# Gate stage, out projection and pooling layer rewritten with features on the partitions; group mix multiplied into the value weights on chip

## The reference

```python
def adaln_params(c, w, b):
    shift, scale, gate = split(silu(c) @ w + b, 3)
# layer 0: sliding-window attention (window 128, 16 heads of 64, 4 kv heads), gate width 1024
    q, k, v, g = split(h @ w_in);  o = banded_sink_attention(rope(rms(q)), rope(rms(k)), v, sinks)
    branch = (o * silu(g)) @ w_out
# layer 1: causal pooling over trailing windows 2/4/8/16, one per group of 256 channels
    v, g = split(h @ w_in)                                   # 1024 + 1024
    pooled = window_sum(v) / count - v                       # per group
    mixed = einsum('bsgc,gcd->bsgd', pooled, w_group) * scale   # 256x256 per group
    branch = (mixed * silu(g)) @ w_out
x = x + gate * branch        # h = rms_norm(x, norm_g) * (1 + scale) + shift
```

## Time and profile before

| | |
|---|---|
| three timed runs | 1764.85, 1769.49, 1775.3 us; median 1769.49 |
| span of the profiled execution | 1762.8 us |
| its own time | not listed apart; the lowest of the timed runs is 2.1 us above the span, the median 6.7 |
| mean granted clock of PE | 0.961 |
| gate and out projection, pooling, last projection | 399.9, 469.0, 198.0 us |

### The profile page before, as it was taken

How to read it: one execution, slowest core, us unless ns; L and a number is a source line. 1 busy time by engine, 2 the same in 40 slices (tenths; PEclk the granted TensorE clock), 3 DMA queues, 4 the chain that set the end, 5 groups by cost and what they waited for, 6 DMA issues and landing times. The chain is left out here.

```text
span 1762.8 us, 27247 instructions
## 1 busy us (share of the span) xinstructions
PE 1581.6 (90%) x9964; PEld 1392.5 (79%) x9964; DVE 920.7 (52%) x1686; ACT 532.0 (30%) x1286; POOL 403.9 (23%) x472
## 2 busy tenths in 40 slices
PE   7579989999898984799999996699999999969998
PEld 3367777777777774699999994689999999957887
DVE  1467766777667763543333333664544545434333
ACT  0255555555555543411100011431221221121000
POOL 0225555555545552010000001111101111000000
PEclk9799999999999986899999998799999999989999
DMA  8331111111111102844333442530111101044332
GB/s 333 113 128 49 73 48 71 48 48 71 48 71 48 59 14 90 283 147 147 143 148 152 155 156 89 173 99 29 42 42 42 48 18 42 19 137 160 148 145 107
DMA packets 75507, 175.36 MB, mean 99 GB/s; under 512 B 11330, under 2 KB 41026, under 8 KB 70212
## 3 DMA queue, kind: packets, MB, share of 16 engines
q1 hardware_dynamic: 71268, 161.60, 25.3%
q0 software_dynamic: 4192, 13.12, 2.2%
HBM read 124.36 MB, written 50.34 MB: 99 GB/s over the span
## 5 line engine op out<-in xcount | busy, mean ns | idle before, releaser
L828 PE MATMUL at_proj<-w_qkv,at_ht 128*128 128x512 f32 x1152 | 286.7, 398 | 11.8 <-DVE at_ht L629 7.2
L828 PEld LDWEIGHTS at_proj<-w_qkv,at_ht 128*128 128x128 f32 x1152 | 211.4, 190 | 60.0 <-DVE at_ht L629 8.2
L1237 PE MATMUL gp_g_ps<-gp_ht,gp_w_g 128*128 128x256 f32 x1536 | 187.4, 285 | 15.7 <-DMA gp_ht<-ht_split 15.7
L1237 PEld LDWEIGHTS gp_g_ps<-gp_ht,gp_w_g 128*128 128x128 f32 x1536 | 187.0, 194 | 16.6 <-DMA gp_ht<-ht_split 16.0
L1630 PE MATMUL po_v_ps<-po_ht,po_w_vg 128*128 128x256 f32 x1536 | 191.3, 286 | 9.4 <-DVE po_ht L1506 9.4
L1630 PEld LDWEIGHTS po_v_ps<-po_ht,po_w_vg 128*128 128x128 f32 x1536 | 188.2, 194 | 11.2 <-DVE po_ht L1506 5.9
L1808 PE MATMUL pj_y_ps<-pj_w_o,pj_zs 128*128 128x512 f32 x768 | 180.6, 397 | 16.8 <-DVE pj_w_o L70 15.2
L1630 PE MATMUL po_g_ps<-po_ht,po_w_vg 128*128 128x256 f32 x1536 | 190.0, 283 | 0.0
L1255 PE MATMUL gp_y_ps<-gp_w_o,gp_zt 128*128 128x512 f32 x768 | 181.3, 395 | 7.3 <-DVE gp_zt L1163 7.3
L1808 PEld LDWEIGHTS pj_y_ps<-pj_w_o,pj_zs 128*128 128x128 f32 x768 | 147.0, 192 | 50.2 <-DVE pj_zs L1768 12.5
L1630 PEld LDWEIGHTS po_g_ps<-po_ht,po_w_vg 128*128 128x128 f32 x1536 | 186.5, 192 | 0.0
(11 more groups left out here) (176 smaller groups left out, 2009.8 us busy)
## 6 DMA issues: line engine op xcount, KB each, us to landing
ht_split<-at_ht SPq DMA_DIRECT2D x16, 1024.0 KB, 3.8
gp_ht<-ht_split SPq DMA_DIRECT2D x16, 1024.0 KB, 6.7
pr_ada<-in_ada_w SPq DMA_DIRECT2D x8, 1536.0 KB, 9.1
gp_ada<-in_ada_w POOLq DMA_DIRECT2D x48, 256.0 KB, 3.1
at_x<-in_x SPq DMA_DIRECT2D x16, 512.0 KB, 3.7
attn_out_t<-at_ot SPq DMA_DIRECT2D x16, 512.0 KB, 2.8
gp_ot<-attn_out_t SPq DMA_DIRECT2D x16, 512.0 KB, 8.1
gp_x<-in_x SPq DMA_DIRECT2D x16, 512.0 KB, 3.3
```

Of the source, the lines that this page charges most:

```text
L828: last = nc.tensor.matmul(proj[:, b * BANK:(b + 1) * BANK], ht[:, s, k, :], w_qkv[:, mv, k, b * BANK:(b + 1) * BANK], start=(k == 0 and (s ...
L1237: last = nc.tensor.matmul(g_ps[:, j, c * 2 * P:(c + 1) * 2 * P], w_g[:, w, k, f * P:(f + 1) * P], ht[:, :, m, k, :], start=(i == 0), stop= ...
```

## The change

The first two stages keep their work. What follows them is now three stages in which activations always have features on the partitions and tokens as columns.

- Inputs. x also comes transposed (`xt`), the output leaves transposed, and the weights of the two out projections and of the pooling layer come in columns of 128 output features (`by_columns`), all laid out before the launch.
- `gates` (stage 1): the gate banks as before, still 256 tokens per step, but the product with the attention output is split and stored to memory (`z_d`, 2 MB per step). The out projection isn't done here. After every second step PE does `fold`: for one group, value weights (transposed) times group weights, 48 matmuls of 256 columns, whose result ACT copies and POOL's queue stores (`wp_d`). The adaLN row is summed as before, six `add_ada` per step, twelve in step 6, and ends as columns `mod1` through 24 matmuls with one column.
- `out_attention` (stage 2): `w_out` stays on chip; 4 blocks of 512 tokens, 8 output chunks each, 24 matmuls of 512 columns per chunk. The residual is one DVE operation. Norm and modulation for layer 1 are done here: ACT squares, POOL adds, PE sums over the partitions with a column of ones (`sum_squares`) and spreads the result (`spread`), DVE scales and splits. x and the split h go to memory.
- `pool_layer` (stage 3): two blocks of 1024 tokens, each as two halves of 512. Per block 24 weight columns (8 value, 8 gate, 8 output) are streamed, split anew each time (`w` has two buffers, `raw` three), and used for both halves: 24 matmuls of 512 columns for each half. The mix is in the value weights already. The gated result `zt` stays on chip for the output columns.

Core of the diff (the new bodies, cut):

```diff
-def gate_and_project(nc, x_v, w_in, w_out, ada_w, ada_b, norm_g, gates_d, ht_d, ot_d, x1_d, ...):
+def gates(nc, w_in, ada_w, ada_b, norm_g, wvt, w_group, wp_d, ht_d, ot_d, z_d, c_silu, mod1, ...):
+                def load_h(s, b):
+                    wait(sp, g_done, PAIRS * s)
+                    sp.dma_start(ht[:, b]..., ht_d[2 * s + b]).then_inc(ht_loaded[b], 16)
+                def load_o(s, b):
+                    wait(sp, z_done, PAIRS * s)
+                def store(s):
+                    sp.wait_ge(zlo_done, PAIRS * (s + 1))
+                    sp.dma_start(z_d[s], zt[:, s % 2]...)
+                for s in range(1, NS):                      # SP
+                    for b in range(2): load_h(s, b)
+                    for b in range(2): load_o(s, b)
+                    store(s - 1)
...
+                for k in range(KC):                         # POOL's queue
+                    if k % 2 == 0: load_pair(k // 2)        # value and group weights of one group
+                    for j in range(MODS):
+                        wait(pool, ada_added, MODS * k + j - 1)
+                        pool.dma_start(ada[:, j % 2, :], ...)
+                    if k % 2 == 1 and k > 1: store_fold(k // 2 - 1)
...
+                for s in range(NS):                         # ACT
+                    tanh(s, 0)
+                    for j in range(PAIRS):
+                        if j + 1 < PAIRS: tanh(s, j + 1)
+                        z_hi(s, j)
+                    if s % 2 == 0: hi_pair(s // 2)
+                    else: fold_evict(s // 2)
...
+                for s in range(NS):                         # DVE
+                    gated / z_lo for the four pairs
+                    if s % 2 == 0: lo_pair(s // 2)
+                    if s < NS - 1:
+                        for j in range(MODS): add_ada(s, j)
+                        if s == NS - 2:
+                            for j in range(MODS): add_ada(NS - 1, j)
...
+                for s in range(NS):                         # PE
+                    for j in range(PAIRS): gate_pair(s, j)
+                    if s % 2 == 1: fold(s // 2)
+                sum_mods()
+
+def out_attention(nc, xt_d, w_out, gates_d, z_d, x1t_d, h1_d, mod1, ident, KC, NB, D):
+                load_w(0); load_z(0); load_w(1); load_w(2); (gate); load_x(0); ...     # SP
+                def load_z(s):
+                    wait(sp, y_done, KC * (s - 1))
+                    for i in range(2):
+                        sp.dma_start(zt[:, s % 2, :, :, i * 2 * P:(i + 1) * 2 * P], z_d[2 * s + i]...)
...
+                for s in range(NSB):                        # PE
+                    for d in range(KC):
+                        out_chunk(s, d)
+                        if s > 0 and d == 1: sum_squares(s - 1)
+                        if s > 0 and d == 2: spread(s - 1)  # waits for POOL's rstd(s - 1)
+                sum_squares(NSB - 1); spread(NSB - 1)
...
+                for s in range(NSB):                        # DVE; STATS_AT = 2
+                    for d in range(KC):                     # H_AT = ((), (), (), (0,), (1, 2), (3, 4), (5, 6), (7,))
+                        residual(s, d)
+                        if s > 0:
+                            if d == STATS_AT: mean(s - 1)
+                            modulate(s - 1, H_AT[d])        # scale_x(k), lo(k - 1)
+                mean(NSB - 1); modulate(NSB - 1, range(KC))
+
-def pool(...) ... -def project(...)
+def pool_layer(nc, w_value, w_gate, w_out, scale_d, x1t_d, h1_d, mod1, out_d, ...):
+        for what, g in (("v", 0), ("v", 1), ("g", 0), ("v", 2), ("g", 1), ("v", 3), ("g", 2), ("g", 3)):
+            USES += [(what, GC * g + c) for c in range(GC)]
+                load_w(0); load_h(0, 0); load_w(1); load_h(0, 1); load_w(2)            # SP
...
+                for b in range(NBLK):                       # DVE
+                    for j, (what, c) in enumerate(USES):
+                        if what == "g":
+                            for h in range(HALVES): silu(b, c, h)
+                        lo_w(i + 2)
+                        if what == "v" and c % GC == GC - 1:
+                            for h in range(HALVES): windows(b, c // GC, h)
+                        if what == "g" and c % GC == GC - 1:
+                            for h in range(HALVES): result(b, c // GC, h)
+                            for h in range(HALVES): lo_z(b, c // GC, h)
+                    for d in range(KC):
+                        for h in range(HALVES): residual(b, d, h)
+                        lo_w(i + 2)
...
+                def front(b, i, what, c):                   # PE
+                    pe.wait_ge(w_lo, i + 1)
+                    for h in range(HALVES):
+                        if i % PER_BLK == 0: pe.wait_ge(h_loaded[h], 16 * (b + 1))
+                        wait(pe, v_out if what == "v" else silu_done, unit(b, c, h) - 1)
+                        # 24 matmuls: bank[:, h, :] <- w[:, i % 2, a, k, :], ht[:, h, m, k, :]
+                def back(b, i, d):                          # the same with zt, and for d == 0:
+                            if k % GC == 0: pe.wait_ge(z_lo, window(b, k // GC, h) + 1)
```

More of the change, by code:

```diff
@@ new lines, in spread @@
+                def spread(s):
+                    pe.wait_ge(rstd_done, s + 1)
+                    wait(pe, hx_done, KC * (s - 1))
+                    for t in range(PER):
+                        last = nc.tensor.matmul(bc_ps[:, s % 2, t * P:(t + 1) * P], rstd[:, s % 2, t:t + 1].to_broadcast([P, P]), ident[:, :],
+                                                start=True, stop=True)
+                    last.then_inc(bc_done, 1)
+                for s in range(NSB):
+                    for d in range(KC):
+                        out_chunk(s, d)
+                        if s > 0 and d == 1:
+                            sum_squares(s - 1)
+                        if s > 0 and d == 2:
+                            spread(s - 1)
@@ L1348, in pool @@
-        load_w, hi_w, lo_w, n_chunks, w_done = split_chunks(ctx, nc, "po", chunks, [w_stage[:, i, :] for i in range(4)])
-        parts = [range(0, ready["mix", 0]), range(ready["mix", 0], ready["mix", 1]),
-                 range(ready["mix", 1], ready["mix", 2]), range(ready["mix", 2], n_chunks)]
-        def x_bank(b, r):
-            return (tr, v_ps)[b][:, r, :]
-        SUMS = sum(g + 3 for g in range(GROUPS))
+        v_ps, g_ps, y_ps = (ctx.enter_context(nc.psum_tensor("po_" + n, [P, 2, BANK], F32)) for n in ("v_ps", "g_ps", "y_ps"))
@@ L1570, in step @@
-                def step(s, more, split=lambda part: None):
-                    for g in range(GROUPS):
-                        if g > 0:
-                            split(g)
-                        windows(s, g)
-                        if g == 2 and more:
-                            modulate(2 * s + 2, 0)
-                            modulate(2 * s + 3, 1)
-                        if g > 0:
-                            silu(s, g - 1)
-                        lo(s, g)
-                        if g > 0:
-                            result(s, g - 1)
-                    if more:
-                        transposed(s + 1)
-                    silu(s, GROUPS - 1)
-                    result(s, GROUPS - 1)
@@ L1588, in _ @@
-                modulate(0, 0)
-                lo_w(dve, 0)
-                modulate(1, 1)
-                for k in parts[0][1:ready["value", 1]]:
-                    lo_w(dve, k)
-                transposed(0)
-                for k in parts[0][ready["value", 1]:]:
-                    lo_w(dve, k)
-                step(0, True, split)
-                nc.vector.memset(fix[:, :, :], 1.0).then_inc(scaled, 1)
-                dve.wait_ge(scaled, 2)
-                with dve.Fori(1, NS - 1) as s:
-                    step(s, True)
@@ L1659, in _ @@
-                uses = {"value": values, "gate": gates, "mix": mix}
-                def step(s, more):
-                    for what, g in USES:
-                        if more and (what, g) == ("gate", GROUPS - 1):
-                            transposes(s + 1)
-                        if isinstance(s, int) and s == 0:
-                            pe.wait_ge(w_done, ready[what, g])
-                        uses[what](s, g)
-                transposes(0)
-                step(0, True)
-                with pe.Fori(1, NS - 1) as s:
-                    step(s, True)
```

1137 lines of the change are left out of this document (579 added, 558 removed).

## The result

| | before | changed | forecast |
|---|---|---|---|
| median, same chip | 1772.26 us | 1852.58 us (1848.81 to 1854.09) | 1801 (1757 to 1835) |
| ratio | 1 | 1.0469 [1.0436, 1.0501] | |
| span of the profiled execution | 1762.8 | 1852.4 | |
| up to the gate stage | 695.9 | 698.8 | unchanged |
| gate stage | | 334.7 | 278 |

They sum to 1153.6 where 1098 was forecast: 55.6 us too many, the gate stage alone 56.7. With 2.9 us before it that is 58.5 of the span; my forecast had added 6.7 us between span and median where 0.2 is found, which leaves, but for rounding, the 51.6 by which the median missed.

What follows compares the result with a forecast made beforehand. PE was taken to set the time. Gate stage 278, out projection 227 and pooling layer 593 sum to 1098 us against 1066.9; the difference, +31, added to the median gave 1801 us (1757 to 1835).

Steps and rivals of the forecast that it cites:

- In the other three the fold fills most: 7.5 us in all, fold included.: Gate stage: at three of seven step transitions the fold fills most of the hidden-row load gap, 7.5 us each.
- 18.4 us to the next stage's first DMA: End of the gate stage: VectorE's backlog, the last fold copies and small sums take 18.4 us, bounds 12 and 24.
- Bare gaps, 7.4 + 1.9 each: Gate stage: four transitions without a fold wait 7.4 us for hidden rows and lose 1.9 us of clock each.
- Out projection, 227: The out projection stage: start 17 + 1.9, matmuls 175.5, three waits of 3.4, end 22.9; sum 227 us.
- My 305: Out projection start: z in 1 KB pieces loads at 305 GB/s, 13.7 us, 17 with weights, issue and landing.
- Pooling layer, 593: Pooling layer with output: start 21.9, matmuls 526.5, silu waits 23.6, their clock 4 x 1.9, turns, end 4.3; sum 593 us.
- 68 saved: PE's matmuls in the rewritten stages: 909 us in all against about 977, 68 us saved.
- D: Rival: out projection bound by DMA at 260 instead of 305 GB/s, 48 us a block; 1821, up to 1840; chance 0.15.
- C: Rival: ends and starts at the stage changes cost 32 us instead of 82; 1751 us; chance 0.13.
- B: Rival: no clock fall in short pauses, z loads at full rate, VectorE's windows begin earlier; 1769 us; chance 0.17.
- E: Rival: a 512-column matmul costs two of 256, 0.240 us, so 17.6 us is not saved; 1819 us; chance 0.05.
- PE busy time falls by 50 to 70 us: Sign to look for in the profile: PE busy time falls 50 to 70 us, its share from 90% to about 85%.

Runs made afterwards that it cites:

- e1: The changed kernel with only the stores of the folded weights moved from GpSimd's queue to SyncE's: 1804.67 us, ratio 1.0186.
- e5: The changed kernel with only VectorE's order in the gate stage changed, the 48 adaLN additions spread between the gated pairs: 1813.78 us, ratio 1.0270.
- e2: The changed kernel with only the pooling layer's window sums of the second half moved one item later on VectorE: 1817.21 us, ratio 1.0274.
- e11: e10 with the fourth pair's low part ahead of the adaLN additions in odd steps: 1724.80 us, ratio 0.9753.
- e9: The changed kernel with e1, e2, e5 and two hidden-row buffers, and in odd steps all adaLN additions behind the fourth gated pair: 1738.35 us, ratio 0.9826.
- e10: e9 with the first loads of the out projection and the pooling layer in two halves: 1731.84 us, ratio 0.9785.

## Why the forecast was right in direction and short in size

- **The failed step: "In the other three the fold fills most: 7.5 us in all, fold included."** True of step 1 only. Steps 3 and 5 took 29.3 us each (833.05 to 862.37; 917.95 to 947.23): 2 x 21.8 = 43.6 us missed. I had written for step 7 that the fold's copies wait on ScalarE behind VectorE's backlog, but never asked what `fold_evict` waits for, namely the store of the fold before, and behind what on GpSimd's queue that store stands. e1 removed just these two waits, with the lower clock in the matmuls behind them, and gave 48 us. e5 left the store where it was, took VectorE's batch apart, and they went as well.
- **"18.4 us to the next stage's first DMA" (bounds 12 and 24): mis-sized, 30.4** (1003.12 to 1033.54). The mechanism was right. The twelve additions ended 37 us after step 6's last bank instead of 30: they took 28.9 us where twice the old six would be 21.3. In e5, without the batch, the same end takes 17.8 us. VectorE alone; the last addition, the first of the gated pairs held up behind them, and the copy of the modulations, 3.9 us ahead of the next stage:

```profile
1006.87 0.75 DVE L1154 SCALAR_TENSOR_TENSOR ga_sums<-ga_ada,c_silu,ga_sums 128x512 f32<-128x512 f32 x1 [1.21 <-DMA ga_ada<-in_ada_w]
1007.54 0.68 DVE L1136 SCALAR_TENSOR_TENSOR ga_t<-ga_t,ga_g_ps 128x512 f32<-128x512 f32 x1
...
1029.69 0.17 DVE L1181 COPY mod<-ga_mod_ps 128x8 f32<-128x8 f32 x1 [12.26 <-PE ga_mod_ps L1224]
```

  I had priced an addition's wait by the old stage, where the transfers moved 160 GB/s on average against 205 here; that the traffic is the reason is not shown. Together these two make 55.6 of the gate stage's 56.7 too many; the start (12.5 for 14) and small losses nearly cancel.
- **Bare gaps, 7.4 + 1.9 each: right.** 7.34 to 7.45 us, runs behind them 24.6 to 25.5 where 23.2 is the full-clock time. The clock as forecast, in the windows from the end of the gap ahead of 808.59 on (0.50, then 0.89):

```profile
808.00:811.00 3.00, 2.41 (x11) 2.44 (x12) 2.57 (x4) 0.00 (x0) 0.69 (x2) 0.50 0.98 264
811.00:814.00 3.00, 3.00 (x25) 3.00 (x24) 0.00 (x0) 0.00 (x0) 0.41 (x1) 0.89 1.08 426
```

- **Out projection, 227: 233.1.** Start 14.5 instead of 17. While it loads z in pieces of 1 KB (4.2 MB of the 5.0 that move before the first product; most of the rest is weights) the transfers run at 385 to 396 GB/s:

```profile
1036.00:1040.00 4.00, 0.00 (x0) 0.00 (x0) 1.23 (x1) 1.06 (x1) 0.00 (x0) 0.50 1.06 385
...
1044.00:1048.00 4.00, 0.00 (x0) 0.00 (x0) 0.00 (x0) 0.00 (x0) 0.00 (x0) 0.50 1.09 396
```

  My 305 came from a stretch in which several kinds of transfer ran side by side; a mixed stretch prices no single one. The Trainium skill, "DMA: Bandwidth & Descriptors", section "Specifications", says that pieces of 512 B or more suffice for line rate. This trace agrees, in that the 1 KB pieces come within 5% of the 402 GB/s that was the highest rate in the earlier trace rows, and the 14 us at that rate was the better figure. The middle was 5 us longer and the end 25.7 for 22.9, so the terms cancel to +6.
- **Pooling layer, 593: 585.8.** The waits for silu were 1.21, 3.76 and 6.29 us, and 0.99, 3.54 and 6.06 in block 1, where 1.4, 3.9 and 6.5 stood; the turns 2.60 each for 2.9. e2 confirms the waits for silu and the clock behind them: 30.2 us in this stage against my 23.6 + 7.6. The turns stayed as they were. The rest is the start (19 for 21.9) and 0.2267 us a matmul instead of 0.2285.
- **The matmuls.** Halving the count at double the width saved 3072 x 0.120 - 1536 x 0.2267 = 20 us. (An estimate by "TensorE: Matmul & The Clock Gate", section "Back-to-back issue gap", of the Trainium skill, N/2.4 + 2.5 ns, gives 4. The trace disagrees and decides: over N/2.4 a matmul takes 13 ns at both widths, 11 more than by that rule.) My "68 saved" was a slip in the sum: the parts listed, 17.6 + 46.1 + 20 - 23.0, give 61, since the new total of 909 leaves out the 6 us of small sums. They stand in the end of the gate stage, so that 1098 is not touched.
- **The rivals.** D (out projection bound by DMA) fell: the start is 14.5 us, and in the middle PE waits only for rstd, 2.0 us three times, and for no transfer. C (hand-overs cheap) fell: the four took 30.4, 14.5, 25.7 and 19 us, 90 in all where I had 82. B fell: the clock dropped in each bare gap. E fell with the row above. "PE busy time falls by 50 to 70 us" was wrong (25.7): besides the slip of 7, I had left out of that figure the time of matmuls at the lower clock and the norm's small sums (10.4 us), which I had counted among the waits.
- In short, a forecast of +31 in which 43.6 us of a chain that I had not seen were missing and 12 us of one that I had seen and priced too low. The range took in the unknown sizes of the waits that I had found and nothing for one that I had not.

What stays open: what lengthened e5's gaps for hidden rows (no run takes traffic away from them), and the 3 us wait ahead of step 3 in e11. Neither was tried further.

## What to carry to other kernels

When a stage loses the work that kept engines apart, follow each buffer's release through every queue it stands in: an eviction waits for a store, the store for its place in a queue, the queue for loads whose consumer blocks. A blocking batch of small operations on one engine is cheap only while nothing else stands behind it; spread between the others, the same instructions here took 52 us out of four waits, and e5 as a whole is 39 us faster. And gains of waits that stand in for each other don't add: the second buffer gave 10 us of 38 with the batch and 22 without it.

## What the runs showed of the hardware that I had not expected

What a pause costs afterwards does not follow from its length alone. Behind one of about 3 us (e9: 3.02 and 3.22) a run of 192 matmuls took 24.8 us, as much as behind one of 7.4; but in e10 the run behind a pause of 3.34 us took 23.3 and lost nothing, while in e5 one behind 1.98 us took 24.7. Behind 1.0 us (e11) nothing was lost, 384 taking 46.3. The same step in e9 and in e10:

```profile
851.40 24.76 PE L1203 MATMUL ga_g_ps<-ga_ht,ga_w_g 128*128 128x256 f32 x192 [3.02 <-DMA ga_ht<-ht_split]
```

```profile
855.94 23.27 PE L1203 MATMUL ga_g_ps<-ga_ht,ga_w_g 128*128 128x256 f32 x192 [3.34 <-DMA ga_ht<-ht_split]
```

Transfers that were mostly pieces of 1 KB moved at 385 to 396 GB/s.
